# Where the operands of fp32r products begin: both on a 64-byte line for 512 columns, half a line apart for 256

## The reference, cut to what matters

```python
x = x + 0.5 * swiglu_ffn(rms_norm(x, g1), w_in, w_out)     # (silu(h @ gate) * (h @ up)) @ w_out, 2816 wide
proj = rms_norm(x, g2) @ w_mix_in                           # then recurrence and attention on its columns
x = x + concat([y_rwkv, y_moba]) @ w_mix_out
x = x + memory_cross_attention(rms_norm(x, g3), rms_norm(mem, g4), w_q, w_kv, w_o)
x = x + 0.5 * swiglu_ffn(rms_norm(x, g5), w_in, w_out)
```

## The kernel before, in words

| stage | weights_split | act | hidden or y | columns |
|---|---|---|---|---|
| feed-forward, first block | 32 | 0 | mlp_hidden 32 | 512 (last down step 256) |
| mixing, memory | 32 | 0 | y 32 | 256 |
| second block | 0 | 0 | mlstm_y 0 | 256 |
| experts | 0 | slot 0 | hidden 32 | 512 |
| experts, to slots and back | 0 | slot 0 | selection 32, select_back 0 | 512 and 128; 256 |

## Time and profile before

### The profile page before, as it was taken

One profiled execution on the slowest core, in us unless ns is written; L12 is line 12 of the kernel. 1 busy time (PEld: TensorE's weight loads), 2 busy tenths in 40 slices (PEclk: granted clock), 3 DMA queues, 4 the chain that ended last, 5 costly groups with the idle time before them and its releaser, 6 DMA issues. The chain is left out here.

```text
span 2014.2 us, 34340 instructions
## 1 busy us (share of the span) xinstructions
PE 1957.0 (97%) x14152; PEld 1702.1 (85%) x14152; DVE 1431.4 (71%) x1858; ACT 1088.7 (54%) x1637; POOL 337.2 (17%) x187
## 2 busy tenths in 40 slices
PE   7999998999999999999989999998999989999999
PEld 5888987999888888889879988887998987888887
DVE  5884775675676567666756667745776668999997
ACT  5444673554544544457555454434655447777775
POOL 1660006000264036300230006600000000000000
PEclk9999999999999999999999999998999979999999
DMA  9655330443665556544115355554333319999994
GB/s 391 261 218 189 137 119 24 148 171 134 230 242 206 188 209 251 188 149 165 64 59 195 144 210 213 226 190 113 126 126 123 139 44 352 373 367 373 373 373 189
DMA packets 56246, 402.46 MB, mean 200 GB/s; under 512 B 6360, under 2 KB 6544, under 8 KB 7840
## 3 DMA queue, kind: packets, MB, share of 16 engines
q1 hardware_dynamic: 51504, 370.74, 48.8%
q0 software_dynamic: 4592, 29.58, 4.3%
HBM read 399.23 MB, written 1.06 MB: 199 GB/s over the span
## 5 line engine op out<-in xcount | busy, mean ns | idle before, releaser
L286 DVE TENSOR_TENSOR weights_split<-ring,weights_split 128x1024 fp32r<-128x1024 f32 x696 | 929.9, 1378 | 166.7 <-ACT weights_split L276 166.3
L276 ACT CAST weights_split<-ring 128x1024 fp32r<-128x1024 f32 x696 | 694.5, 1050 | 225.1 <-PE ps L303 210.0
L301 PE MATMUL ps<-weights_split,act_hi 128*128 128x512 f32 (+1 forms) x960 | 356.6, 371 | 12.6 <-DVE weights_split L286 12.4
L303 PE MATMUL ps<-weights_split,act_lo 128*128 128x512 f32 (+1 forms) x960 | 350.3, 365 | 0.0
L302 PE MATMUL ps<-weights_split,act_hi 128*128 128x512 f32 (+1 forms) x960 | 350.3, 365 | 0.0
L301 PE MATMUL ps<-act_hi,weights_split 128*128 128x256 f32 x992 | 292.0, 294 | 1.1 <-DVE act_lo L3178 0.9
L302 PE MATMUL ps<-act_lo,weights_split 128*128 128x256 f32 x992 | 283.9, 286 | 0.0
L303 PE MATMUL ps<-act_hi,weights_split 128*128 128x256 f32 x992 | 283.6, 286 | 0.0
L301 PEld LDWEIGHTS ps<-weights_split,act_hi 128*128 128x128 f32 x960 | 181.0, 189 | 44.6 <-DVE weights_split L286 12.4
L303 PEld LDWEIGHTS ps<-weights_split,act_lo 128*128 128x128 f32 x960 | 180.7, 188 | 32.5
L302 PEld LDWEIGHTS ps<-weights_split,act_hi 128*128 128x128 f32 x960 | 181.0, 189 | 29.8
(11 more groups left out here) (532 smaller groups left out, 3037.9 us busy)
## 6 DMA issues: line engine op xcount, KB each, us to landing
ring<-stream SPq DMA_DIRECT2D x348, 1024.0 KB, 4.9
stretch<-ada_in POOLq DMA_DIRECT2D x24, 1024.0 KB, 5.3
act_lo_room<-mem_in SPq DMA_DIRECT2D x2, 1024.0 KB, 4.9
consts<-w_consts SPq DMA_DIRECT2D x1, 1376.0 KB, 11.8
x<-x_in SPq DMA_DIRECT2D x1, 1024.0 KB, 4.9
stretch<-mem_in POOLq DMA_DIRECT2D x1, 1024.0 KB, 9.6
bias_t<-bias_scratch POOLq DMA_DIRECT2D x1, 1024.0 KB, 10.8
out<-x SPq DMA_DIRECT2D x4, 256.0 KB, 2.1
```

The lines of the kernel that those rows point to most:

```text
L276: core.nc.scalar.copy(self.hi[:, self.place(i), part], core.slot(chunk)[:, part]).then_inc(self.rounded.sem, 1)
L286: core.nc.vector.tensor_tensor(self.lo[:, self.place(i), part], core.slot(chunk)[:, part], self.hi[:, self.place(i), part].bitcast(F32), A ...
L301: nc.tensor.matmul(out, lhs[0], rhs[0], start=start, stop=False, **kw)
L303: return nc.tensor.matmul(out, lhs[1], rhs[0], start=False, stop=stop, **kw)
```

## The change

Tiles that are operands of fp32r products get an explicit place in the 64-byte line. `phased` allocates a tile with up to 15 elements of padding ahead of it, so that it begins at byte 0 (EVEN) or 32 (ODD) of a line; `shared` does so with byte 0 for the tiles that also have a plain float32 view. No instruction is added, removed or put elsewhere in its engine's order; only addresses differ, and later tiles in SBUF move up by the padding.

```diff
+LINE = 64
+EVEN, ODD = 0, 32
...
+def lined(columns, at, shape):
+    axes = "abcd"[:len(shape) - 1]
+    sizes = {axis: k for axis, k in zip(axes[1:], shape[2:])}
+    return columns[:, at:at + math.prod(shape[1:])].rearrange(f"p ({' '.join(axes)}) -> p {' '.join(axes)}", **sizes)
...
+    def phased(self, name, shape, dt, ctx, phase):
+        at = -(-self.nc.sbuf_base // 32) * 32
+        pad, n = (phase - at) % LINE // 4, math.prod(shape[1:])
+        room = self.sb(name, [P, pad + n], dt, ctx=ctx)
+        return lined(room, pad, shape)
...
# Splitter: weights_split at byte 0
-        self.room, pair = core.shared("weights_split", [P, self.WAYS, 2, CCOLS], F32R, ctx)
+        shape = [P, self.WAYS, 2, CCOLS]
+        self.room, pair = (lined(t, 0, shape) for t in core.shared("weights_split", math.prod(shape[1:]), F32R, ctx))
...
# ffn_stage
-        hid_hi = core.sb("mlp_hidden_hi", [P, 2, 2, S], F32R, ctx=ctx)
+        hid_hi = core.phased("mlp_hidden_hi", [P, 2, 2, S], F32R, ctx, EVEN)
...
# expert_stage: slot, selection, hidden EVEN
+        a_hi = core.phased("slot_hi", [P, TILES, KB, SLOTS], F32R, ctx, EVEN)
+        back = core.phased("select_back", [P, TILES, S], F32R, ctx, ODD)
+        select = core.phased("selection", [P, TT, TILES * SLOTS], F32R, ctx, EVEN)
+        hid_hi = core.phased("hidden_hi", [P, 2, 2, SLOTS], F32R, ctx, EVEN)
...
# memory_stage, second_stage
+        hi, lo = (core.phased(name, [P, KB, S], F32R, ctx, ODD) for name in ("y_hi", "y_lo"))
+        hi, lo = (core.phased(name, [P, KB, S], F32R, ctx, ODD) for name in ("act_hi", "act_lo"))
+        ym = tuple(core.phased(name, [P, 4, S], F32R, ctx, ODD) for name in ("mlstm_y_hi", "mlstm_y_lo"))
...
# build: one room for act of the first block, used at either place
+            def normed(name, layer, turn, sq=h, begun=6, order=tuple(range(KB)), phase=ODD):
+                hi, lo = (lined(t, phase // 4, [P, KB, S]) for t in (act_hi, act_lo))
+                return LateNorm(core, (hi, lo, norm_sum, norm_rs), x, core.param(name, layer), sq, turn, begun, order)
-            mlp = normed("ffn1_norm_g", 0, "mlp", begun=0)
+            mlp = normed("ffn1_norm_g", 0, "mlp", begun=0, phase=EVEN)
-                mlp = normed("ffn2_norm_g", layer, "mlp")
+                mlp = normed("ffn2_norm_g", layer, "mlp", phase=EVEN)
```

More of the change, by code:

```diff
@@ L7 @@
+import math
 from contextlib import ExitStack
@@ L169, in sb, with shared @@
         return (ctx or self.ctx).enter_context(self.nc.sbuf_tensor(f"{name}_{self.names[name]}", shape, dt))
-    def shared(self, name, shape, dt, ctx):
+    def phased(self, name, shape, dt, ctx, phase):
         at = -(-self.nc.sbuf_base // 32) * 32
-        room = self.sb(name + "_room", shape, ctx=ctx)
-        return room, self.nc.alloc_sbuf_tensor_at(f"{name}_{self.names[name + '_room']}", shape, dt, offset=at)
+        pad, n = (phase - at) % LINE // 4, math.prod(shape[1:])
+        room = self.sb(name, [P, pad + n], dt, ctx=ctx)
+        return lined(room, pad, shape)
+    def shared(self, name, n, dt, ctx):
+        at = -(-self.nc.sbuf_base // 32) * 32
+        pad = -at % LINE // 4
+        room = self.sb(name + "_room", [P, pad + n], ctx=ctx)
+        typed = self.nc.alloc_sbuf_tensor_at(f"{name}_{self.names[name + '_room']}", [P, n], dt, offset=at + 4 * pad)
+        return room[:, pad:pad + n], typed[:, :]
     def sig(self, name, n, of_dma=False):
@@ L345, in ffn_stage @@
             prod = stretch[:, 5120:5632].rearrange("p (t n) -> p t n", t=TT)
-        hid_hi = core.sb("mlp_hidden_hi", [P, 2, 2, S], F32R, ctx=ctx)
-        hid_lo = core.sb("mlp_hidden_lo", [P, 2, 2, S], F32R, ctx=ctx)
+        hid_hi = core.phased("mlp_hidden_hi", [P, 2, 2, S], F32R, ctx, EVEN)
+        hid_lo = core.phased("mlp_hidden_lo", [P, 2, 2, S], F32R, ctx, EVEN)
         block = core.block
@@ L1830, in expert_stage @@
         token_hi, token_lo = (t[:, 2, :].rearrange("p (t n) -> p t n", t=TT) for t in (weights.hi, weights.lo))
-        a_hi = core.sb("slot_hi", [P, TILES, KB, SLOTS], F32R, ctx=ctx)
-        a_lo = core.sb("slot_lo", [P, TILES, KB, SLOTS], F32R, ctx=ctx)
-        back = core.sb("select_back", [P, TILES, S], F32R, ctx=ctx)
+        a_hi = core.phased("slot_hi", [P, TILES, KB, SLOTS], F32R, ctx, EVEN)
+        a_lo = core.phased("slot_lo", [P, TILES, KB, SLOTS], F32R, ctx, EVEN)
+        back = core.phased("select_back", [P, TILES, S], F32R, ctx, ODD)
         lg = core.sb("router_logits", [P, TT, G + EXPERTS], ctx=ctx)
@@ L1842, in expert_stage @@
         slot_share = core.sb("slot_share", [P, TILES, E], ctx=ctx)
-        select = core.sb("selection", [P, TT, TILES * SLOTS], F32R, ctx=ctx)
-        hid_hi = core.sb("hidden_hi", [P, 2, 2, SLOTS], F32R, ctx=ctx)
-        hid_lo = core.sb("hidden_lo", [P, 2, 2, SLOTS], F32R, ctx=ctx)
+        select = core.phased("selection", [P, TT, TILES * SLOTS], F32R, ctx, EVEN)
+        hid_hi = core.phased("hidden_hi", [P, 2, 2, SLOTS], F32R, ctx, EVEN)
+        hid_lo = core.phased("hidden_lo", [P, 2, 2, SLOTS], F32R, ctx, EVEN)
         work = h[:, :, :].rearrange("p k t -> p (k t)")
@@ L2270, in memory_stage @@
         weights.of_stage(start)
-        hi, lo = (core.sb(name, [P, KB, S], F32R, ctx=ctx) for name in ("y_hi", "y_lo"))
+        hi, lo = (core.phased(name, [P, KB, S], F32R, ctx, ODD) for name in ("y_hi", "y_lo"))
         mem_hi, mem_lo = acts.hi, acts.lo
@@ L2690, in second_stage @@
         weights = Splitter(core, ctx, start, n)
-        hi, lo = sb("act_hi", [P, KB, S], F32R), sb("act_lo", [P, KB, S], F32R)
-        ym = sb("mlstm_y_hi", [P, 4, S], F32R), sb("mlstm_y_lo", [P, 4, S], F32R)
+        hi, lo = (core.phased(name, [P, KB, S], F32R, ctx, ODD) for name in ("act_hi", "act_lo"))
+        ym = tuple(core.phased(name, [P, 4, S], F32R, ctx, ODD) for name in ("mlstm_y_hi", "mlstm_y_lo"))
         branch_gate = sb("branch_gate", [P, 16, S])
@@ L3518, in build @@
             core.rest = core.sig("inputs_loaded", 16 * len(rest), of_dma=True)
[L3519 to L3524, removed]
+            act_room, act_lo = core.shared("act_lo", KB * S + ODD // 4, F32R, first)
+            b.act_room = lined(act_room, ODD // 4, [P, KB, S])
+            act_hi = core.phased("act_hi", [P, KB * S + ODD // 4], F32R, first, EVEN)
+            norm_sum, norm_rs = core.sb("norm_sum", [P, S], ctx=first), core.sb("norm_rs", [P, TT], ctx=first)
+            def normed(name, layer, turn, sq=h, begun=6, order=tuple(range(KB)), phase=ODD):
+                hi, lo = (lined(t, phase // 4, [P, KB, S]) for t in (act_hi, act_lo))
+                return LateNorm(core, (hi, lo, norm_sum, norm_rs), x, core.param(name, layer), sq, turn, begun, order)
             run = ExitStack()
             weights = Splitter(core, run, STREAM_AT["ffn1", 0][0], 3 * FFN_STEPS + 13)
-            mlp = normed("ffn1_norm_g", 0, "mlp", begun=0)
+            mlp = normed("ffn1_norm_g", 0, "mlp", begun=0, phase=EVEN)
             for layer in range(DEPTH):
@@ L3541, in build @@
                 rwkv_stage(core, layer, b, weights, query, h, y)
-                mlp = normed("ffn2_norm_g", layer, "mlp")
+                mlp = normed("ffn2_norm_g", layer, "mlp", phase=EVEN)
                 memory_stage(core, layer, b, weights, query, mlp, x, h, y)
-                following = normed("ffn1_norm_g", layer + 1, "mlp_after", order=BLOCK_ORDER) if more else None
+                following = normed("ffn1_norm_g", layer + 1, "mlp_after", order=BLOCK_ORDER, phase=EVEN) if more else None
                 ffn_stage(core, ("ffn2", layer), FFN_STEPS, weights, x, mlp, h,
```

## The result

The changed kernel takes 2006.84 us (median of 6 runs, 2005.27 to 2008.86), the kernel before 2018.07 beside it: ratio 0.9942, 95% interval 0.9931 to 0.9954. That is 11 us less. The forecast was 20 us less and a range that ended at 2004, so time and range missed; the direction was right. The profiled execution took 2006.15 us (before 2015.99).

What follows compares the result with a forecast made beforehand. TensorE was taken as the bound nearly everywhere. Gains summed to 21.4 us, less 5% 20.3, taking the profiled 2015.99 to 1995.7 us; with 0.2 for the median the forecast was 1996 us, range 1989 to 2004.

Steps and rivals of the forecast that it cites:

- Part 1: Feed-forward gate and up products, 2112 matmuls of 512 columns: 233.4 to 227.4 ns each, 12.7 us gained.
- distance or bank: Rival of no gain: costs follow something else differing between tiles, unchanged by moving all 32 bytes; 2016.2 us, chance 0.05.
- Part 2: Down products of the experts, 480 matmuls: from 232 to 233.4 down to 227.4 ns, 2.5 us gained.
- Part 3: `mlp_hidden` and slot products keep the same place: 0, with up to 1 us over 1920 matmuls left to the range.
- Part 4: y products, 768 matmuls: 119.9 to 117.5 ns, between two half-line costs differing in role and byte; 1.8 us gained.
- Part 5: Second block, 1440 products of 256 columns: 120.0 to 117.5 ns, taken as 3.2 us gained.
- Part 6: Mixing and memory products with act, 1824 moving act and 576 moving weights: 1.0 us gained, ends 0 and 2.0.
- Part 7: `select_back`, 80 products: 0.2 us gained; `selection`, a few dozen: 0.
- Part 8: Padding moves later tiles; fp32 products of the recurrence change their places relative to each other, costed at nothing.
- only the 512-column part works: Rival: 256-column differences belong to which tiles meet; 14.4 us gained, 2001.8 us, chance 0.10.
- T3: Experts' products: what counts is the streamed operand against the stationary one loaded meanwhile; moving all lo parts keeps 227 to 228.
- R3: Experts' products, rival: what counts is each moving operand against its own stationary operand; moving all lo parts gives 230 to 233.

Runs made afterwards that it cites:

- e_all256: Changed kernel with act hi and lo at 0/0 from the weights modulo 256 in feed-forward parts, 32/32 in mixing and memory: 1994.45 us, ratio 0.9885.
- k_ffn_act_alone: Kernel before with only act of the feed-forward parts moved, by 32 bytes, to 0/0 against the weights modulo 256: 2003.69 us, ratio 0.9948.
- j_weights_lo_alone: Only the lo part of the experts' weights moved 64 bytes, slot and hidden kept, other act places swept, against e_all256's layout: 2015.11 us, single run.
- f_sweep: e_all256 with other act places in feed-forward, mixing and memory, and the experts' slot_lo moved by 128 bytes: 2010.9 us, single run.
- g_lo_with_lo: Lo parts of the experts' weights, slot and hidden all moved 64 bytes, other act places swept, against e_all256's layout: 2011.0 us, single run.
- experiment 3: g_lo_with_lo and j_weights_lo_alone, on which operand counts against which: 2011.0 and 2015.11 us. Its third reading: any jump of place between successive products costs something.

## Why the prediction was wrong

- *What bounds the kernel*: right. TensorE's gaps nearly stayed, and what its spacings lost the kernel lost.
- *Part 1, gate and up products, 12.7 us*: the step that failed. Summed from start to start, these 2112 matmuls went from 499.4 to 497.1 us, 2.3 us less. The prediction sorted pairs by their place in a 64-byte line, took act at 0 and weights at 0 to be like slot and weights, and priced them at 227.4. But slot and weights agreed modulo 256, and act came to -64/-128. The four pairs on which it rested could not tell 64 from 256 bytes, since all fast ones happened to be at 0/0 and all slow ones at -32/-32. With act at 0/0 the same products took 488.7 us, 10.7 less (`e_all256`), 11.1 less in `k_ffn_act_alone`; so the term was sound for the right places, if 1.6 to 2.0 us too high, and was applied to the wrong ones. The prediction had named this among its rivals, as distance or bank, but for a case with no gain at all and at one in twenty.
- *Part 2, the experts' hidden, 2.5 us*: right, 2.8 measured (111.7 to 108.9 us). The stage went from 343.9 to 340.6 us with DMA at 351 GB/s and VectorE at 91.4% (349 and 90.8% by the earlier trace rows), so neither DMA nor VectorE held it. The prediction's spacing before, 232, was a little low: the mean over all was 233.2 in dense stretches.
- *Part 3, 0 to 1 us*: 1.2 measured.
- *Part 4, y, 1.8 us*: 2.1 measured. What was left open, role or byte, was neither: moving minus stationary at +32 costs 116.7, at -32 118.3. Both were in the trace, but a line of 64 bytes makes +32 and -32 the same.
- *Part 5, second block, 3.2 us*: the spacing of act moving fell as was said, 120.0 to 116.6 in the window shown and from 119.7 to 117.2 in the rest; weights moving fell less, 119.6 to 118.3. Over the counts of the prediction that is 3.6 us. The sum over these products fell by 6.0 us. The rest, 2.4 us, is scatter: in `k_ffn_act_alone`, where their places were those of before, the sum also fell, by 1.9, and from the last product of the feed-forward part to the first slot product it took 282.2 to 287.1 us in the nine kernels with the changed places and 285.2 to 288.2 in the three with the old ones. TensorE's granted clock over 1370 to 1640 us differs from run to run, 0.92 to 0.95. The kernel before had 0.94 there in its trace and the changed one 0.95; one hundredth of these 270 us is 2.7 us, an estimate from two rounded figures, but of the size of the 2.4:

```profile
1370.00:1640.00 270.00, 255.10 (x1881) 0.94 0.35 121
1370.00:1640.00 270.00, 252.79 (x1903) 0.95 0.36 121
```

- *Part 6, mixing and memory with act, 1.0 us*: wrong in sign. They lost 1.5 us, with act_hi and act_lo apart there as well (-32/-96). In `e_all256`, at 32/32, they gained 2.7.
- *Part 7, `select_back`, 0.2 us*: right, its products went from 119.8 to 116.7 ns. They are in "all else" below.
- *Part 8, the recurrence, 0*: all else lost 2.9 us in this trace, mostly at fp32 products of the recurrence: `h` by `weights_split_room` 1.1 us, `consts` by it 1.0, `stretch` by it 0.8. Places don't explain it. The first falls in a stretch of the changed kernel at half of the full clock, in which these products were spaced 193 ns instead of 90; before, there was no such stretch there (the windows are those of the changed kernel, then of the kernel before):

```profile
354.70:357.90 3.20, 3.20 (x49) 0.50 0.02 5
354.10:357.30 3.20, 2.92 (x111) 1.00 0.03 5
```

`j_weights_lo_alone`, in whose trace the same stretch is at half clock, shows the same 1.1 us, and `e_all256`, which gives these operands the same places as `j_weights_lo_alone`, does not. Of the other two, most is one interval each, 680 ns before and 1229 after for `consts`, 691 and 1506 for `stretch`; in `e_all256`, `f_sweep`, `g_lo_with_lo` and `j_weights_lo_alone`, where these operands lie alike, they vary from 678 to 953 and from 418 to 1447.

The bill: -2.3 - 2.8 - 1.2 - 2.1 - 6.0 + 1.5 + 2.9 = -10.0, and the span fell from 2014.2 to 2004.3 us. That the two scatters, 2.4 gained in part 5 and 2.9 lost in part 8, nearly cancel is luck. Of the rivals, "only the 512-column part works" had it the wrong way round: y and the second block gained with 256 columns, and act with 512 hardly did.

## What to carry to other kernels

Before a rule is read from a few fast and slow pairs, list every address bit in which they differ; here pairs half a line of 64 bytes apart were apart modulo 256 too, and only the second reading held. In this kernel fp32r products of 512 columns cost 2.4% less than before (227.6 against 233.2 ns) when the stationary operand's hi and lo parts and the weights all begin at the same place modulo 256 bytes, and a helper that pads a tile must say the place of each part, not of the first alone. A control that should change nothing (here 128 bytes more) can be the run that tells most. Why the place matters no run shows: of the theories about which operand meets which, T3 fell, and R3 is not parted from the third reading in experiment 3.

## What the runs showed that was not expected

- A step as fine as 4 bytes changes the spacing: 227.6 ns at 0, 232.3 at 4, 230.7 at 8, the last two each from one feed-forward part.
- No place of the sweep brought 512 columns under what 0/0 costs; `slot` and `mlp_hidden` have means up to 228.6 there.
- 256 columns at a distance of 64 run at 113.4 or 117.8 ns with the same code and places in two layers, the lowest spacing and a middling one.
